# Stick-breaking attention with the queries on the partitions, on one Trainium2 core

## The chip, the cores and the metric

One NeuronCore of a Trainium2 chip runs the whole kernel. The metric is the device time of one execution in microseconds (us). Engines are named as in the profile: PE (TensorE), ACT (ScalarE), DVE (VectorE), POOL (GpSimd) and SP (SyncE, which here only issues DMAs).

## What is computed

One layer of a hybrid decoder on 1024 prompt tokens and 8 decode tokens (TT = 1032 columns), in fp32. The change lies in branch C, the stick-breaking attention of the prompt (4 heads of 128). With strict causality, key k counts for query q only where k < q:

```
z = (jnp.einsum('bqhd,bkhd->bhqk', q, k).astype(jnp.float32) * (SB_HEAD_DIM ** -0.5)
     + bias.astype(jnp.float32)[None, :, None, None])
mask = k_pos[None, :] < q_pos[:, None]
log_keep = jnp.where(mask, jax.nn.log_sigmoid(-z), 0.0)
later = lax.cumsum(log_keep, axis=3, reverse=True) - log_keep
a = jnp.where(mask, jnp.exp(jax.nn.log_sigmoid(z) + later), 0.0)
return jnp.einsum('bhqk,bkhd->bqhd', a.astype(v.dtype), v)
```

So a = sigmoid(z) times the product of sigmoid(-z) over all later keys up to the query. k and v of the prompt and of the decode tokens are outputs too. The same stage also projects the columns of branch B (a gated causal convolution of width 3) and of a merge gate.

## The kernel before, in words

The kernel is a row of stages (blocks) with a barrier after each: normalise the input, project_attention, stick_breaking_prompt, then the mLSTM, the merge and the feed-forward stages, which the change leaves alone.

*Projection.* Every projection works in blocks of 128 output columns. SP loads 512 KB of weights (load_weights), POOL splits them into a rounded part and a remainder (split_weights, L106 and L109), PE multiplies (project_chunk, L136): a block is three chunks of 344 token columns, a chunk is 24 products (8 slices of 128 input features, each as high x high, high x low, low x high). ACT copies a chunk out of PSUM. Weight buffers alternate, so the split of block n + 1 starts when block n - 1 is done.

*project_attention* (L345) projects q, k and v of four heads, 12 blocks, into s_T, feature-major.

*stick_breaking_prompt* (L423) runs over four heads (loop variable j). In a head it projects four more blocks, 12 chunks, and the 12 chunks are the slots between which the attention's own work is laid. A head has 12 units (UNITS): half 0 has key blocks 3 to 0, half 1 has 7 to 0; a unit is one block of 128 keys on the partitions by up to 512 queries. A unit goes through the engines in this order:

- PE scores (L506): z, keys on the partitions, fp32.
- ACT softplus_log (L568 to L574) and DVE softplus_parts, softplus_sum, split_softplus (L647 to L671): softplus of z, masked on the diagonal, split into a high and a low part, sp_hi and sp_lo.
- POOL add_later and split_later (L736 to L757): the running sum over the later key blocks, split too.
- PE sums (L514, L520): products with triangles and with minus ones, which add the sums of the later keys to z in PSUM.
- ACT probs (L582): exp; POOL mask_prob (L764) on diagonal units.
- PE values (L529): one fp32 product of v_tok with up to 512 columns of prob, added into y.

PE's order is written out by hand in the slot loop at L535: chunk(slot), scores(slot - 1), sums(slot - 2), values(slot - 3). A head has 15 such slots, the last three without a chunk. At slot 0 turn_kv (L486) turns the head's v and k, which ACT staged (L587, L589), token-major; they are stored from there. DVE also runs the convolution (L715, L680 to L685, L720).

## Time and profile before

| | |
|---|---|
| runs | 2289.34, 2289.61 and 2295.07 us, median 2289.61 |
| the profiled execution | span 2287.8 us from its first to its last instruction |
| PE, busy share of the span | 92% |
| DVE, ACT, POOL | 40%, 22%, 33% |
| project_attention | PE's products from 43.93 to 181.4 us |
| stick_breaking_prompt | from 184.5 us; the next stage's first product at 544.09 us |

Times in the rows are us from the span's start. A busy share says little where products overlap: the profile shows a product of 344 columns as 0.32 us long, though the next starts 0.16 us later. The waits say which engine PE stood still for, and the granted clock at which of its levels it ran.

### The profile page before, as it was taken

The numbers are of one execution on the slowest core, as the hardware profiler recorded it, in microseconds if no ns is written. First come the engines' busy times: TensorE is split into PE (matmuls) and PEld (weight loads), VectorE is DVE, ScalarE is ACT, GpSimd is POOL, SyncE is SP. The second block draws the span as 40 slices with busy tenths as digits, with TensorE's granted clock in tenths as the row PEclk, the third lists the DMA queues.
The fourth block names the chain that finished last, engine by engine and source line by source line (L and its number), as shares of the span: only waits on it lengthen the run. The fifth ranks groups of instructions, "written<-read, shape, count | busy, mean of one in ns | idle before, by whom it ended". The sixth has DMA issues, their size and how long they took to land. (4 is left out here: it accounts for less than half of the span.)

```text
span 2287.8 us, 36641 instructions
## 1 busy us (share of the span) xinstructions
PE 2112.9 (92%) x12796; PEld 2020.3 (88%) x12796; DVE 924.2 (40%) x1515; ACT 493.9 (22%) x929; POOL 760.0 (33%) x585
## 2 busy tenths in 40 slices
PE   7999798897999989996999999999999999997797
PEld 6998687686898979996899989999999999997787
DVE  3003655655346435663546443312412312344423
ACT  4113343341111112221213122101101200212321
POOL 5334564553232212220224323333333333332441
PEclk9999899998999989998889999999999999998898
DMA  6112112113343235552644402111111111111012
GB/s 187 46 37 65 53 39 64 55 28 121 98 123 111 74 120 156 156 152 85 208 148 125 148 20 64 46 46 46 46 46 46 46 46 46 46 46 49 26 39 91
DMA packets 238683, 182.41 MB, mean 80 GB/s; under 512 B 15730, under 2 KB 212474, under 8 KB 238508
## 3 DMA queue, kind: packets, MB, share of 16 engines
q1 hardware_dynamic: 221356, 158.60, 24.2%
q10 hardware_dynamic: 17280, 23.22, 2.9%
q8 instruction: 26, 0.43, 0.1%
q14 instruction: 21, 0.17, 0.0%
HBM read 147.69 MB, written 34.12 MB: 79 GB/s over the span
## 5 line engine op out<-in xcount | busy, mean ns | idle before, releaser
L136 PE MATMUL acc<-x_hi,w_hi 128*128 128x344 f32 x2688 | 887.0, 330 | 41.7 <-DVE x_lo L1867 15.7
L136 PE MATMUL acc<-x_lo,w_hi 128*128 128x344 f32 x2688 | 866.1, 322 | 0.0
L136 PE MATMUL acc<-x_hi,w_lo 128*128 128x344 f32 x2688 | 865.3, 322 | 0.0
L106 POOL TENSOR_SCALAR w_hi<-w_raw 128x1024 fp32r<-128x1024 f32 (+2 forms) x176 | 189.9, 1079 | 1275.5 <-PE acc L136 1081.9
L136 PEld LDWEIGHTS acc<-x_hi,w_hi 128*128 128x128 f32 x2688 | 512.6, 191 | 59.8 <-issue 26.1
L136 PEld LDWEIGHTS acc<-x_lo,w_hi 128*128 128x128 f32 x2688 | 511.8, 190 | 6.6 <-issue 5.4
L136 PEld LDWEIGHTS acc<-x_hi,w_lo 128*128 128x128 f32 x2688 | 511.6, 190 | 0.0
L109 POOL TENSOR_TENSOR w_lo<-w_raw,w_hi 128x1024 fp32r<-128x1024 f32 (+2 forms) x176 | 399.3, 2269 | 14.7
L136 PE MATMUL acc<-z_hi,w_hi 128*128 128x344 f32 x768 | 246.5, 321 | 0.0
L136 PE MATMUL acc<-z_hi,w_lo 128*128 128x344 f32 x768 | 245.5, 320 | 0.0
L136 PE MATMUL acc<-z_lo,w_hi 128*128 128x344 f32 x768 | 245.3, 319 | 0.0
L1812 DVE TENSOR_TENSOR h<-acc,h 128x344 f32 (+1 forms) x120 | 61.7, 514 | 310.6 <-PE acc L136 310.6
L2039 ACT ACTIVATE relu_sq<-relu 128x344 f32<-128x344 f32 x96 | 47.3, 492 | 551.5 <-DVEq L2006 551.5
L136 PEld LDWEIGHTS acc<-z_hi,w_hi 128*128 128x128 f32 x768 | 144.6, 188 | 0.2 <-issue 0.2
L136 PEld LDWEIGHTS acc<-z_lo,w_hi 128*128 128x128 f32 x768 | 144.4, 188 | 0.2 <-issue 0.2
L136 PEld LDWEIGHTS acc<-z_hi,w_lo 128*128 128x128 f32 x768 | 144.5, 188 | 0.0
L2002 DVE SCALAR_TENSOR_TENSOR relu<-acc,sq_sum 128x344 f32<-128x344 f32 x96 | 49.4, 515 | 209.1 <-PE acc L136 209.1
L136 PE MATMUL acc<-y_hi,w_hi 128*128 128x344 f32 x288 | 99.0, 344 | 32.4 <-DVE y_lo L1713 29.9
L1993 DVE TENSOR_TENSOR x_lo<-relu_sq,x_hi 128x344 f32 x96 | 95.7, 1010 | 29.4 <-issue 29.4
L136 PE MATMUL acc<-y_lo,w_hi 128*128 128x344 f32 x288 | 98.2, 341 | 0.0
L136 PE MATMUL acc<-y_hi,w_lo 128*128 128x344 f32 x288 | 97.6, 339 | 0.0
L136 PEld LDWEIGHTS acc<-y_hi,w_hi 128*128 128x128 f32 x288 | 59.3, 206 | 37.5 <-DVE y_lo L1713 22.8
(303 smaller groups left out, 2140.5 us busy)
## 6 DMA issues: line engine op xcount, KB each, us to landing
w_raw<-in_w_in SPq DMA_DIRECT2D x64, 512.0 KB, 4.3
page<-in_cache_k SPq DMA_DIRECT2D x64, 256.0 KB, 2.9
v_page<-in_cache_v SPq DMA_DIRECT2D x64, 256.0 KB, 2.7
w_raw<-in_w_up SPq DMA_DIRECT2D x32, 512.0 KB, 4.1
w_raw<-in_w_down SPq DMA_DIRECT2D x32, 512.0 KB, 3.7
merge_gate<-merge_gates SPq DMA_DIRECT2D x24, 516.0 KB, 3.8
merge_gates<-gate_out ACTq DMA_DIRECT2D x16, 516.0 KB, 3.3
y_raw<-branch_outputs SPq DMA_DIRECT2D x9, 688.0 KB, 6.7
```

The costliest lines, as they stand in the source:

```text
L106: nc.gpsimd.tensor_scalar(k.w_hi[:, par, 0:kb, :], k.w_raw[:, par, 0:kb, :], 1.0, 1.0, ALU.mult, ALU.mult).then_inc(k.w_rounded, 1)
L109: nc.gpsimd.tensor_tensor(k.w_lo[:, par, 0:kb, :], k.w_raw[:, par, 0:kb, :], k.w_hi[:, par, 0:kb, :].bitcast(F32), ALU.subtract).then_inc( ...
L136: mm = k.nc.tensor.matmul(k.acc[:, c, 0:CW], w[:, par, i, :], x[:, i, cols], start=(i == 0 and j == 0), stop=(i == kb - 1 and j == 2))
L1812: k.nc.vector.tensor_tensor(out[:, :, cols], k.acc[:, c:c + 1, 0:CW], out[:, :, cols], ALU.add).then_inc(k.acc_free, 1)
L1993: nc.vector.tensor_tensor(u_lo[:, bass.ds(i * 2 + par, 1), c * CW:(c + 1) * CW], square[:, c:c + 1, :], u_hi[:, bass.ds(i * 2 + par, 1), c ...
L2002: nc.vector.scalar_tensor_tensor(out=relu[:, c, :], in0=k.acc[:, c, 0:CW], scalar=0.0, in1=norm.rstd[:, c * CW:(c + 1) * CW], op0=ALU.max, ...
L2039: nc.scalar.activation(square[:, c, :], relu[:, c, :], ACT.Square).then_inc(s["squared"], 1)
```

## The change

Queries are put on the partitions, keys along the free dimension. A unit is now one block of 128 queries by up to four key blocks (still 12 per head, 48 in all, and the same 36 blocks of 128 by 128 per head). ACT makes keep = sigmoid(-z - bias) and beta = sigmoid(z + bias) straight from PSUM. DVE runs one scan along the keys in reversed order (a product of keep, and a maximum with a matrix that puts 1 where the mask ends), which leaves the running product in left, and multiplies beta by it. POOL masks beta on the diagonal block. PE turns the probabilities, block by block, ACT copies them out, and PE multiplies each block by v. The sums over later keys as products, the splits and the chain on POOL are gone. Units run on over the heads without a pause: PE's order per slot is chunk(slot), scores(slot + 1), turn(slot), values(slot - 1).

project_attention projects v first, then k, then q, and turns v and k of a head behind the first chunk of the next block; SP stores them from there. The loops are written out, and ACT's table for the stage holds the sigmoid.

```diff
-def project_attention(k, groups, s_T, then):
+def project_attention(k, s_T, v_tok, then):
...
+    V, KEY, Q = range(3)
+    cols = (C_SV, C_SK, C_SQ)
...
+        def place(n):
+            g, h = divmod(n, H)
+            return v_head[:, h % 2, :] if g == V else s_T[:, (g == KEY) * H + h, :]
...
+                for n in range(1, count):
+                    g, h = divmod(n, H)
+                    load_weights(k, sp, base + n, n % 2, w_in[:, :, cols[g] + h * P:cols[g] + (h + 1) * P])
+                    if 0 <= n - 3 < 2 * H:
+                        store(n - 3)
...
+                def turn(n):
+                    g, h = divmod(n, H)
+                    pe.wait_ge(k.acc_free, (base + n + 1) * NCH + NCH)
+                    if g and h == 0:
+                        pe.wait_ge(s["dec_ready"], g)
+                    tr = nc.tensor.transpose(dec[:, h * P:(h + 1) * P], place(n)[:, T:TT], k.ident[:, :])
+                    if h == H - 1:
+                        tr.then_inc(s["dec_turned"], 1)
+                    if g != Q:
+                        if n >= 2:
+                            pe.wait_ge(s["tok_ready"], n - 1)
+                        for tb in range(TB):
+                            tr = nc.tensor.transpose(turned[:, n % 2, tb // 4, (tb % 4) * P:(tb % 4 + 1) * P],
+                                                     place(n)[:, tb * P:(tb + 1) * P], k.ident[:, :])
+                        tr.then_inc(s["turned"], 1)
+                for n in range(count):
                     for c in range(NCH):
+                        project_chunk(k, pe, base + n, n % 2, c, k.x_hi, k.x_lo)
+                        if c == 0 and n:
+                            turn(n - 1)
+                turn(count - 1)
...
-            pe.wait_ge(k.acc_free, (base + H) * NCH + NCH)
-            for h in range(H):
-                tr = nc.tensor.transpose(turned[:, h * P:(h + 1) * P], s_T[:, h, T:TT], k.ident[:, :])
-            tr.then_inc(q_turned, 1)
...
+                for n in range(2 * H):
+                    g, h = divmod(n, H)
+                    dve.wait_ge(s["turned"], n + 1)
+                    if g == KEY and h >= 2:
+                        dve.wait_ge(k_out[h % 2], 16 * (h // 2))
+                    out = v_tok[:, h, :, :] if g == V else k_tok[:, h % 2, :, :]
+                    nc.vector.tensor_copy(out, turned[:, n % 2, :, :].rearrange("p a (b d) -> p (a b) d", d=P))\
+                        .then_inc(s["tok_ready"], 1)
+                    if h == H - 1:
+                        read_decode(g, kv_dec[:, g, :])
+                read_decode(Q, k.q_tok[:, :])
...
-UNITS = [(half, kb, max(0, kb * P - half * 512)) for half in range(2) for kb in range(4 * half + 3, -1, -1)]
+UNITS = [(h, i, 4 * part, min(i + 1 - 4 * part, 4)) for h in range(H) for i in range(TB) for part in range(i // 4, -1, -1)]
...
+FIRST = [kb0 == 4 * (i // 4) for _, i, kb0, _ in UNITS]
+NFIRST = [sum(FIRST[:u]) for u in range(NU + 1)]
+HALF_END = [u for u in range(NU) if UNITS[u][1] % 4 == 3 and UNITS[u][2] == 0]
...
-                with pe.Fori(0, H) as j:
-                    for slot in range(SLOTS + 3):
-                        if slot < SLOTS:
-                            b, c = divmod(slot, NCH)
-                            project_chunk(k, pe, base + j * NB + b, b % 2, c, k.x_hi, k.x_lo)
-                        if slot == 0:
-                            turn_kv(j)
-                        if 0 <= slot - 1 < NU:
-                            scores(j, slot - 1)
-                        if 0 <= slot - 2 < NU:
-                            sums(j, slot - 2)
-                        if 0 <= slot - 3 < NU:
-                            values(j, slot - 3)
...
+                def scores(u):
+                    h, i, kb, n = UNITS[u]
+                    if u >= 2:
+                        pe.wait_ge(s["beta_ready"], u - 1)
+                    nc.tensor.matmul(z[:, u % 2, 0:n * P], s_T[:, h, i * P:(i + 1) * P],
+                                     s_T[:, H + h, kb * P:(kb + n) * P], start=True, stop=True).then_inc(s["z_ready"], 1)
+                def turn(u):
+                    h, i, kb, n = UNITS[u]
+                    pe.wait_ge(s["prob_ready"], u + 1)
+                    if u >= 2:
+                        pe.wait_ge(s["copied"], u - 1)
+                    for b in range(n):
+                        tr = nc.tensor.transpose(tp[:, u % 2, b * P:(b + 1) * P], prob[:, u % 2, b * P:(b + 1) * P], k.ident[:, :])
+                    tr.then_inc(s["turned"], 1)
+                def values(u):
+                    h, i, kb, n = UNITS[u]
+                    pe.wait_ge(s["copied"], u + 1)
+                    if FIRST[u] and i % 4 == 0 and u:
+                        pe.wait_ge(s["y_read"], sum(e < u for e in HALF_END))
+                    for b in range(n):
+                        mm = nc.tensor.matmul(y[:, (i % 4) * P:(i % 4 + 1) * P], v_tok[:, h, kb + b, :],
+                                              prob_T[:, u % 2, b * P:(b + 1) * P], start=(FIRST[u] and b == 0),
+                                              stop=(kb == 0 and b == n - 1), skip_group_check=True)
+                    mm.then_inc(s["av_done"], 1)
+                scores(0)
+                for slot in range(H * SLOTS):
+                    n, c = divmod(slot, NCH)
+                    project_chunk(k, pe, base + n, n % 2, c, k.x_hi, k.x_lo)
+                    if slot + 1 < NU:
+                        scores(slot + 1)
+                    turn(slot)
+                    if slot:
+                        values(slot - 1)
+                values(NU - 1)
...
+                def sigmoids(u):
+                    h, i, kb, n = UNITS[u]
+                    act.wait_ge(s["z_ready"], u + 1)
                     if u >= 2:
+                        act.wait_ge(s["left_ready"], u - 1)
+                    nc.scalar.activation(keep[:, u % 2, 0:n * P], z[:, u % 2, 0:n * P], ACT.Sigmoid, scale=-1.0,
+                                         bias=neg_bias[:, h:h + 1]).then_inc(s["keep_ready"], 1)
                     if u >= 2:
+                        act.wait_ge(s["turned"], u - 1)
+                    nc.scalar.activation(prob[:, u % 2, 0:n * P], z[:, u % 2, 0:n * P], ACT.Sigmoid,
+                                         bias=k.b_sb[:, h:h + 1]).then_inc(s["beta_ready"], 1)
+                def copy_turned(u):
+                    h, i, kb, n = UNITS[u]
+                    act.wait_ge(s["turned"], u + 1)
+                    if u >= 2:
+                        act.wait_ge(s["av_done"], u - 1)
+                    nc.scalar.activation(prob_T[:, u % 2, 0:n * P], tp[:, u % 2, 0:n * P], ACT.Copy).then_inc(s["copied"], 1)
...
+                sigmoids(0)
+                for slot in range(H * SLOTS):
+                    n, c = divmod(slot, NCH)
+                    j, b = divmod(n, NB)
...
+                    acc_wait(k, act, base + n, c)
+                    nc.scalar.activation(proj[:, b, c * CW:(c + 1) * CW], k.acc[:, c, 0:CW], ACT.Copy).then_inc(k.acc_free, 1)
+                    if slot + 1 < NU:
+                        sigmoids(slot + 1)
+                    copy_turned(slot)
+                    if b == 0 and c == 1 and j:
+                        send_conv(j - 1)
+                    if slot - 2 in HALF_END:
+                        send_y(HALF_END.index(slot - 2))
...
+                def leave(u):
+                    h, i, kb, n = UNITS[u]
+                    lo, hi = kb * P, (kb + n) * P
+                    if u:
+                        dve.wait_ge(s["prob_ready"], u)
+                    if u % SLOTS == 0:
+                        nc.vector.memset(left[:, P:T + 1:P], 1.0)
                         dve.drain()
+                    dve.wait_ge(s["keep_ready"], u + 1)
+                    if FIRST[u]:
+                        masked, start = behind[:, 512 - n * P:512], 1.0
                     else:
+                        masked, start = behind[:, 0:1].to_broadcast([P, 512]), left[:, hi:hi + 1]
+                    nc.vector.tensor_tensor_scan(left[:, lo:hi][:, ::-1], keep[:, u % 2, 0:n * P][:, ::-1], masked[:, ::-1],
+                                                 start, ALU.mult, ALU.max).then_inc(s["left_ready"], 1)
+                    if FIRST[u]:
+                        dve.wait_ge(s["beta_masked"], NFIRST[u] + 1)
+                    else:
+                        dve.wait_ge(s["beta_ready"], u + 1)
+                    dve.wait_ge(s["left_ready"], u + 1)
+                    nc.vector.tensor_tensor(prob[:, u % 2, 0:n * P], prob[:, u % 2, 0:n * P], left[:, lo + 1:hi + 1],
+                                            ALU.mult).then_inc(s["prob_ready"], 1)
+                def read_y(e):
+                    dve.wait_ge(s["av_done"], HALF_END[e] + 1)
+                    if e >= 2:
+                        dve.wait_ge(y_sent[e % 2], 16 * (e // 2))
+                    nc.vector.tensor_copy(y_out[:, e % 2, :], y[:, :]).then_inc(s["y_read"], 1)
...
+                leave(0)
+                for slot in range(H * SLOTS):
+                    j, e = divmod(slot, SLOTS)
+                    if slot + 1 < NU:
+                        leave(slot + 1)
+                    if slot - 1 in HALF_END:
+                        read_y(HALF_END.index(slot - 1))
...
+                def mask_beta(u):
+                    h, i, kb, n = UNITS[u]
+                    pool.wait_ge(s["beta_ready"], u + 1)
+                    nc.gpsimd.affine_select(out=prob[:, u % 2, (n - 1) * P:n * P], in_=prob[:, u % 2, (n - 1) * P:n * P],
+                                            compare_op=ALU.is_gt, fill=0.0, base=0, pattern=[[-1, P]],
+                                            channel_multiplier=1).then_inc(s["beta_masked"], 1)
+                mask_beta(0)
+                for slot in range(H * SLOTS):
+                    n, c = divmod(slot, NCH)
+                    if c == 0:
+                        split_weights(k, pool, base + n + 1, (n + 1) % 2, (base + n + 1) // 2)
+                    if slot + 1 < NU and FIRST[slot + 1]:
+                        mask_beta(slot + 1)
...
-            s_T = k.sb(part, "s_T", [P, 3 * H, TT])
-            project_attention(k, [group(C_SQ, block_of(s_T, 0), HD_SCALE), group(C_SK, block_of(s_T, H)),
-                                  group(C_SV, block_of(s_T, 2 * H))], s_T, w_in[:, :, C_CC:C_CC + P])
-            stick_breaking_prompt(k, s_T, w_in[:, :, C_MQ:C_MQ + P])
+            s_T = k.sb(part, "s_T", [P, 2 * H, TT])
+            v_tok = k.sb(part, "v_tok", [P, H, TB, P])
+            project_attention(k, s_T, v_tok, w_in[:, :, C_CC:C_CC + P])
+            stick_breaking_prompt(k, s_T, v_tok, w_in[:, :, C_MQ:C_MQ + P])
```

The places where instructions move:

PE in project_attention, at the end before and behind the first chunk of the second block after. Before, the stage ends with four turns of the query's decode rows (s_T[:, h, T:TT]) and goes on to the loop of the next stage:

```order
L368 COMPARE_AND_BRANCH
L375 MATMUL q_turned<-ident,s_T 8x128 x4
L355 UNCONDITIONAL_BRANCH
L481 UNCONDITIONAL_BRANCH
L534 UNCONDITIONAL_BRANCH
L534 ISA
```

After, v_head is a head's projected v, kv_turned and rows_turned are PSUM:

```order
L136 MATMUL acc<-x_hi,w_hi 128x344
L136 MATMUL acc<-x_lo,w_hi 128x344
L136 MATMUL acc<-x_hi,w_lo 128x344
L407 MATMUL rows_turned<-ident,v_head 8x128
L414 MATMUL kv_turned<-ident,v_head 128x128 x8
L136 MATMUL acc<-x_hi,w_hi 128x344
L136 MATMUL acc<-x_lo,w_hi 128x344
```

Eight such groups, with v_head and then s_T, have come into the stage from the heads' loop.

PE between two chunks of the stick-breaking stage, in the first slot after slot 1 of the first head whose score has 128 columns. Before:

```order
L506 MATMUL z<-s_T,k_head 128x128
L512 REGISTER_ALU
L514 MATMUL z<-sp_hi,neg_from_r 128x512
L514 MATMUL z<-sp_lo,neg_from_r 128x512
L517 REGISTER_ALU
L520 MATMUL z<-later_hi,neg_ones_r 128x384
L520 MATMUL z<-later_lo,neg_ones_r 128x384
L528 REGISTER_ALU
L529 MATMUL y<-prob,v_tok 128x384
```

After (tp is the turned block in PSUM, sb_prob_T its copy):

```order
L511 MATMUL z<-s_T 128x128
L520 MATMUL tp<-ident,sb_prob 128x128 x4
L529 MATMUL y<-sb_prob_T,v_tok 128x128 x3
```

The four products with the triangle and with minus ones are gone, four turns have come, and the value is three products of 128 columns where it was one of 384.

DVE, one unit of 512 columns. Before (off the diagonal):

```order
L647 TENSOR_SCALAR z_pos<-z,sb_bias 128x512
L654 TENSOR_TENSOR z_abs<-z_pos,z_abs 128x512
L668 REGISTER_ALU
L669 CAST sp_hi<-z_abs 128x512
L671 TENSOR_TENSOR sp_lo<-z_abs,sp_hi 128x512
```

After, two units and the piece of the convolution that stands between the first and the second:

```order
L634 SCALAR_TENSOR_TENSOR sb_left<-sb_keep,sb_behind 128x384
L641 TENSOR_TENSOR sb_prob<-sb_prob,sb_left 128x384
L654 TENSOR_SCALAR proj_out<-cx,conv_w_c 128x1032
L655 COPY cx_tails<-cx 128x10
L634 SCALAR_TENSOR_TENSOR sb_left<-sb_keep,sb_left,sb_behind 128x512
L641 TENSOR_TENSOR sb_prob<-sb_prob,sb_left 128x512
```

Four passes of DVE over a unit (five on the diagonal) have become the scan and one product.

## Rows read from the trace of the kernel before

**Rows 1.** The page, part 1: busy time (share of the span) and instructions.
```profile
PE 2112.9 (92%) x12796; PEld 2020.3 (88%) x12796; DVE 924.2 (40%) x1515; ACT 493.9 (22%) x929; POOL 760.0 (33%) x585
```

**Rows 2.** Windows: stretch, length, busy PE, PEld, DVE, ACT, POOL, PE clock, DMA share, GB/s.
```profile
184.50:539.00 354.50, 307.83 (x1596) 259.98 (x1596) 210.27 (x275) 135.73 (x253) 193.25 (x216) 0.94 0.17 51
```

**Rows 3.** PE's waits, 184.5 to 544 us: total us, times, longest.
```profile
PE z L514 <- DVE sp_lo L671: 37.3, 17, 5.1
PE y L529 <- POOL prob L764: 4.8, 4, 1.2
PE z L491 <- ACT cx L589: 4.6, 3, 2.2
PE acc L136 <- DVE neg_ones_r L642: 2.6, 1, 2.6
```

**Rows 4.** Timeline, PE in head 0: start, length, operation [idle before <-releaser].
```profile
190.52 0.32 PE L136 MATMUL acc<-x_lo,w_hi 128*128 128x344 f32 x1
...
194.14 0.38 PE L506 MATMUL z<-s_T,k_head 128*128 x2
...
216.40 0.38 PE L506 MATMUL z<-s_T,k_head 128*128 x2
...
218.24 0.32 PE L136 MATMUL acc<-x_lo,w_hi 128*128 128x344 f32 x1
...
256.54 1.02 PE L506 MATMUL z<-s_T,k_head 128*128 x2
...
257.85 0.39 PE L520 MATMUL z<-later_hi,neg_ones_r 128*128 128x512 f32 x1
258.08 0.40 PE L520 MATMUL z<-later_lo,neg_ones_r 128*128 128x512 f32 x1
...
259.17 1.02 PE L506 MATMUL z<-s_T,k_head 128*128 x2
```

**Rows 5.** Timeline, PE: turns of a head's v; weight loads of fp32 products, input stage.
```profile
188.40 1.03 PE L491 MATMUL z<-ident,cx 128*128 128x128 f32 x8
189.27 0.27 PE L493 MATMUL z<-ident,cx 128*8 128x128 f32 x1
...
16.96 1.86 PEld L334 LDWEIGHTS pt_s<-x_scales,x_rows 128*128 128x128 f32 x16 [1.62 <-DVE x_scales L292]
18.74 0.91 PEld L326 LDWEIGHTS pt_x<-ident,x_rows 128*128 128x128 f32 x8
```

**Rows 6.** Timeline, DVE and POOL in head 0.
```profile
237.15 0.69 DVE L671 TENSOR_TENSOR sp_lo<-z_abs,sp_hi 128x512 fp32r<-128x512 f32 x1
...
243.55 2.40 POOL L109 TENSOR_TENSOR w_lo<-w_raw,w_hi 128x1024 fp32r<-128x1024 f32 x1
243.78 2.72 DVE L671 TENSOR_TENSOR sp_lo<-z_abs,sp_hi 128x512 fp32r<-128x512 f32 x1
```

**Rows 7.** Timeline, the end of the last head and the next stage's first product.
```profile
529.33 0.63 PE L514 MATMUL z<-sp_lo,neg_from_r 128*128 128x512 f32 x1
...
538.78 0.69 DVE L692 COPY y_stick<-y 128x512 f32<-128x512 f32 x1 [0.92 <-PE y L529]
...
544.09 0.65 PE L136 MATMUL acc<-x_hi,w_hi 128*128 128x344 f32 x1 [4.91 <-PEq L463]
```

**Rows 8.** Groups (count, busy us, mean ns) of ACT and POOL; one DVE instruction, timeline.
```profile
L568 ACT ACTIVATE z_abs<-z,sb_bias 128x512 f32<-128x512 f32 x24 | 16.5, 688 | 8.2 <-PE z L506 8.0
L603 ACT ACTIVATE proj_out<-acc 128x344 f32<-128x344 f32 x48 | 21.9, 457 | 139.5 <-PE acc L136 122.6 <-issue 16.9
L764 POOL TENSOR_SCALAR_AFFINE_SELECT prob<-prob 128x128 f32<-128x128 f32 x32 | 13.4, 418 | 0.0
...
270.68 3.38 DVE L683 SCALAR_TENSOR_TENSOR proj_out<-cx,conv_w_c,proj_out 128x1024 f32<-128x1024 f32 x1
```

**Rows 9.** Timeline, PE: the first product of two stages.
```profile
43.93 0.65 PE L136 MATMUL acc<-x_hi,w_hi 128*128 128x344 f32 x1 [2.03 <-PEq L229]
...
184.52 0.42 PE L136 MATMUL acc<-x_hi,w_hi 128*128 128x344 f32 x1 [2.57 <-DVE neg_ones_r L642]
```

More of the change, by code:

```diff
@@ L444, in stick_breaking_prompt @@
-        later_lo = k.sb(ctx, "later_lo", [P, 512], F32R)
-        neg_from = k.sb(ctx, "neg_from_r", [P, P], F32R)
-        neg_ones = k.sb(ctx, "neg_ones_r", [P, P], F32R)
-        later = k.sb(ctx, "sp_later", [P, 512])
-        prob = k.sb(ctx, "prob", [P, 2, 512])
-        y_out = k.sb(ctx, "y_stick", [P, T])
+        keep = k.sb(ctx, "sb_keep", [P, 2, 512])
+        prob = k.sb(ctx, "sb_prob", [P, 2, 512])
+        left = k.sb(ctx, "sb_left", [P, T + 2])
+        prob_T = k.sb(ctx, "sb_prob_T", [P, 2, 512])
@@ L463, in stick_breaking_prompt @@
+        y_sent = [k.sem(ctx, f"sb_y_sent{i}") for i in range(2)]
         with nc.Block() as block:
@@ L634, in _ @@
+                send_conv(H - 1)
+                send_y(2 * H - 1)
+                for i in range(2):
+                    act.wait_ge(y_sent[i], 16 * H)
+                act.wait_ge(s["conv_sent"], 16 * H)
+                act.wait_ge(s["gate_sent"], 16 * H)
             @block.vector
             def _(dve):
[L636 to L639 removed]
```

411 lines of the change are left out of this document (107 added, 304 removed).

## The prediction

> **What bounds the kernel now.** The page comes first: TensorE (PE) is busy 92% of the span of 2287.8 us [rows 1], so only time in which PE waits, runs at its lower clock or does work that can be dropped is worth anything. Both stages that the change touches lie before 544.09 us. The windows show the stick-breaking stage: from 184.5 to 539 us, 354.5 us, PE is busy 307.83 us at a mean granted clock of 0.94 [rows 2]. The waits name what holds it [rows 3]: 37.3 us in 17 waits of the sums (L514) for sp_lo from DVE, 4.8 us for the mask on POOL, 4.6 us for the staged head, and before the stage 2.6 us for a constant. The rest of the gap is the clock: a 128x512 product that takes 0.39 us takes 0.63 us at 529.33 [rows 4, 7], after PE had waited for sp_lo. A mean of 0.94 between 1.0 (2.4 GHz) and 0.5 (1.2 GHz) is 12% of 354.5 us at the lower level, half of which is lost: 21 us.
>
> **Prices on PE**, all at the higher level.
> - Projection: 23 products from 190.52 to 194.14 [rows 4], 0.1574 us each; a chunk of 24 is 3.78 us.
> - 512 columns: a single-pass product is 0.23 us (257.85 to 258.08). The unit from 256.54 to 259.17, 2.63 us, has four of these and two fp32 ones (score and value) [rows 4]; (2.63 - 0.92) / 2 = 0.85 us, or 0.21 per 128 columns.
> - Turning a 128x128 block: eight from 188.40 to 189.27 [rows 5], 0.109 us each.
> - An fp32 product of 128 columns that loads its own weights: eight pairs of loads from 16.96 to 18.74 [rows 5], 0.2225 us each.
> - Coming back to the projection: from 216.40 to 218.24 less one product of 0.157 is 1.68 us; the parts (score 0.21, sums 0.46, later sums 0.35, value 0.64) make 1.66 [rows 4]. So 0.02; I take 0.1 per slot for the new kinds, which change weights every 128 columns, and keep 0 and 0.2 as ends.
>
> A head has 12 units, 36 blocks of 128 keys by 128 queries, before and after. Before, its extra PE work is 36 x (0.21 + 0.21) = 15.3, sums 36 x 2 x 0.058 = 4.2, later sums 28 x 2 x 0.058 = 3.2, turning k and v about 2.0 and 0.2 for returns: 25, with 12 chunks 70.4. Four heads: 281 us. With the waits inside the stage (46.7) and the clock (21) that makes 349 of the 354.5 us, so nothing large is missing.
>
> **The change, part by part.**
> 1. *Stick stage, PE.* Sums and later sums go; 36 blocks are turned; a value product is now one per block. Per head: 36 x 0.2125 + 36 x 0.109 + 36 x 0.2225 + 12 x 0.1 = 7.7 + 3.9 + 8.0 + 1.2 = 20.8 us. With chunks: 4 x (45.4 + 20.8) = 264.6 us.
> 2. *The wait in each slot.* turn(u) needs prob(u). PE issues scores(u) at the end of slot u - 1, then turn(u - 1), values(u - 2), a whole chunk and scores(u + 1) before turn(u). For 512 columns that cover is 0.44 + 0.89 + 3.78 + 0.85 = 5.9 us; its smallest value for such a unit (u = 3, between narrow ones) is 0.33 + 0.45 + 3.78 + 0.21 = 4.8. The chain under it: keep on ACT 0.69 [rows 8], the scan, the product with left 0.69 (the 128x512 operation at 237.15 [rows 6]), and about 0.4 for three or four hand-overs; beta (0.69) runs beside the scan. The scan is in no row. From below it is the 0.69 us of a two-input operation over 512 [rows 6]; from above I take the longest two-input operation shown, 3.38 us over 1024 columns while POOL split weights [rows 8]. That gives a chain of 2.5 to 5.2. I take 1.0 for the scan, nearest its low end since operands and length are those of the short row: chain 2.8, no wait. Only in the four narrow places could the top end show, 0.4 us each. The Trainium skill (DVE: opcode table, instruction layouts, handler registers and perf-mode slots, section 6, Datapath and trigger behaviour) says that the built-in scan runs at half throughput; as an estimate from it the scan is some 1.3 us, and the sum stays what it is. No run here shows it yet.
> 3. *What else is queued.* ACT per slot: projection copy 0.46 [rows 8], two sigmoids and the copy of the turned block, at most 0.46 + 3 x 0.69 = 2.5 us, against 5 us or more of PE. send_conv, send_y and the gates only issue DMAs whose work is finished slots earlier. DVE: the convolution pieces and read_y come behind leave(u + 1), whose result is due about 4 us later. POOL loses its chain and keeps the weight splitting and eight masks per head. SP's loads keep their order. All this I cost at nothing; its cover is the chunk of 3.78 us.
> 4. *Ends of heads.* Before, each head drains its pipeline in three slots without a chunk, and those waits are in rows 3. After, units run on across heads, and the pipeline drains once; values(46), 0.89 us, covers the last copy.
> 5. *Exit.* From the last copy of y (538.78) to the next stage's first product (544.09) is 5.31 us [rows 7]; this chain (copy, tails, two small stores, barrier) stays. With 0.3 us from the last value product: 5.6.
> 6. *Attention stage.* Eight k/v blocks are turned there: 8 x (8 x 0.109 + 0.11) = 7.9; the query rows 0.3 more; 11 returns of 0.1: 1.1. The last turn now waits for ACT's last copy (0.46 us [rows 8]), in place of the four turns that stood at the end: even. Sum +9.3. turn(n - 1) stands behind chunk 0 of block n, so the copies it needs are done by then; stores of k and v now queue on SP between weight loads that are due two blocks later.
> 7. *Stage start.* 2.57 us of idleness that ended with neg_ones_r [rows 9] becomes a plain stage change, 2.03 us in the place before the attention stage, plus the first score 0.2: -0.3.
>
> **Sum.** From the first projection product at 184.52 to 544.09 is 359.6 us; now 264.6 + 5.6 = 270.2. -89.4 + 9.3 - 0.3 = **-80.4 us**. The profiled span of 2287.8 becomes 2207.4; the median of the runs, 2289.6, lies 1.8 above the span, so **2209 us**.
>
> **The rivals.**
> *A. POOL holds the scans.* In every third slot the split of the next weights starts when a block ends, just as that slot's unit goes through DVE. The trace shows what this does: the same operation takes 0.69 us at 237.15 and 2.72 beside the split at 243.78 [rows 6]. If scan and product are both held so, each 2.0 us longer, and the mask (0.4 [rows 8]) stands between them, the chain is 2.8 + 4.4 = 7.2 us against 5.9: 1.3 us in each of 16 slots, 21 us, **2230**. For it: both new operations read two SBUF operands, as the held one does. Against it: the split is 3.4 us long in all, so two full holds hardly fit, and the chain's first 0.8 us is ACT's. The Trainium skill (SBUF — State Buffer, Who interferes with whom) states that such a DVE instruction and a GpSimd one that reads SBUF shut each other out for the whole instruction; by that rule A is real, and the row at 243.78 agrees with it.
> *B. The scan is serial and slow; slower than before.* Its elements depend on one another, and it may run far below the rate of a product. A head has six units of 512 columns, the stage 24. Their scan may take 1.0 + (5.9 - 2.8) = 4.1 us before PE waits at all; the gain is gone when each of them waits 80.4 / 24 = 3.35 us, so from a scan of 7.5 us, eleven times the short row. At 9 us, 24 x 4.9 = 118 us come on top: **2327**. PE would idle in front of the turns.
> *C. Straight-line code.* The PE stream has 4530 rows for 2927, since the loops are written out. If fetching it cost the 2.03 us of a stage change [rows 9] once in each of 28 blocks, 57 us return: **2266**. Against it: head 0 runs its body for the first time at 0.1574 us a product.
>
> **How the numbers follow.** Forecast 0.75; A 0.17; C 0.04; B 0.04. About 0.3% (7 us) is what a measurement of this kernel can tell from no change. B is slower: 0.04. A code price 1.4 times C's (80 us) would end within 0.3%: 0.01 of C's share. The rest is faster: 0.95. The forecast's own range: returns of 0 to 0.2 us (4.8 either way) and some 3 us for exit and start, 2201 to 2217. Taking in A with the mask stretched too (to 2238), leaving out B and C: **2200 to 2238**.
>
> **What would show it.** In the new profile: no wait of turn (L520) on sb_prob above 0.5 us; a granted clock of 0.99 from start to end of the stage, and a stage of 265 us from its first score to its last value; the attention stage about 9 us longer; scans of 512 at 0.7 to 1.5 us away from the split. A shows as scans of 2 us or more beside the split, with PE idle in every third slot. B shows as DVE busy without a gap. C shows as PE idle for no releaser, in straight runs of projection. I am wrong if waits at L520 or L529 come to over 30 us, or if the stage exceeds 300 us.

## The result, and the profile after

The change makes the kernel faster: the median is 2195.92 us (2193.39 to 2198.25, 4 runs) against 2289.48 of the kernel before, a ratio of 0.9583, 95% interval 0.9569 to 0.9596. The forecast was 2209, its range 2200 to 2238. Sign and mechanism came out as argued. The size did not: the gain is 93.6 us where the sum had 80.4, and the time lies 4 us under the low end of the range.

PE is the page's first line, to be set beside [rows 1]:

```profile
PE 2073.3 (94%) x12956; PEld 2011.6 (92%) x12956; DVE 846.3 (39%) x1390; ACT 448.0 (20%) x869; POOL 637.8 (29%) x433
```

The windows view, over the attention stage and over the stick-breaking stage from its first projection product to the copy of its last y (columns as in [rows 2]):

```profile
44.00:192.00 148.00, 146.35 (x941) 145.18 (x942) 11.71 (x12) 16.64 (x37) 41.25 (x24) 0.99 0.26 72
192.09:452.40 260.31, 260.31 (x1682) 244.18 (x1682) 119.60 (x142) 90.67 (x193) 73.35 (x64) 1.00 0.18 54
```

In the second stretch PE is busy for 260.31 of 260.31 us, at a granted clock of 1.00, its upper level of 2.4 GHz. In [rows 2] it was 307.83 of 354.5 at 0.94. From the first projection product to the copy of the last y the stage took 354.3 us before (184.52 to 538.78 [rows 7, 9]) and takes 260.3 now, 93.9 less. Of these, 46.7 are the waits inside the stage [rows 3], and some 20 the lower clock, an estimate from the mean of 0.94, of which about 2 fell into waits. The rest, some 29, is PE work that was dropped or has moved to the attention stage. PE's waits between 40 and 480 us, in place of [rows 3] (total us, times, longest):

```profile
PE acc L136 <- PEq L493: 3.7, 1, 3.7
PE z L511 <- PEq L367: 1.0, 1, 1.0
PE acc L136 <- PEq L229: 0.9, 1, 0.9
PE rows_turned L407 <- ACT s_T L451: 0.5, 1, 0.5
```

No wait at the turns (L520) or the value products (L529) is in the list. What remains are changes of stage and the turn of the last query rows. Next the timeline: the turns of two successive blocks in the attention stage, the stage's start, and its exit (rows of several engines between them left out).

```profile
60.82 1.03 PE L414 MATMUL kv_turned<-ident,v_head 128*128 128x128 f32 x8
...
73.14 1.03 PE L414 MATMUL kv_turned<-ident,v_head 128*128 128x128 f32 x8
...
191.88 0.46 PE L511 MATMUL z<-s_T 128*128 128x128 f32 x2 [1.04 <-PEq L367]
...
192.09 0.40 PE L136 MATMUL acc<-x_hi,w_hi 128*128 128x344 f32 x1
...
452.41 0.69 DVE L648 COPY y_stick<-y 128x512 f32<-128x512 f32 x1 [3.38 <-PE y L529]
...
456.47 0.42 PE L136 MATMUL acc<-x_hi,w_hi 128*128 128x344 f32 x1 [3.66 <-PEq L493]
```

And the groups of DVE in the stage (count, busy us, mean ns, idle before):

```profile
L634 DVE TENSOR_TENSOR_SCAN sb_left<-sb_keep,sb_left,sb_behind 128x512 f32<-128x512 f32 x16 | 28.2, 1764 | 55.2 <-ACT sb_keep L559 55.2
L641 DVE TENSOR_TENSOR sb_prob<-sb_prob,sb_left 128x512 f32<-128x512 f32 x24 | 20.0, 832 | 2.6
...
L634 DVE TENSOR_TENSOR_SCAN sb_left<-sb_keep,sb_behind 128x512 f32<-128x512 f32 x8 | 9.8, 1225 | 16.3 <-ACT sb_keep L559 16.3
```

The scan, which no row of before showed, takes 1.23 us over 512 columns, or 1.28 for one that continues a row. The mean of 1764 ns over the 16 continuing ones is above that because four of them, one in each head, ran beside POOL's split of the weights and took 3.20. The one of the first head, with the product and the turn of its unit:

```profile
238.80 2.39 POOL L109 TENSOR_TENSOR w_lo<-w_raw,w_hi 128x1024 fp32r<-128x1024 f32 x1
...
239.06 3.20 DVE L634 TENSOR_TENSOR_SCAN sb_left<-sb_keep,sb_left,sb_behind 128x512 f32<-128x512 f32 x1 [3.23 <-ACT sb_keep L559]
...
242.37 0.69 DVE L641 TENSOR_TENSOR sb_prob<-sb_prob,sb_left 128x512 f32<-128x512 f32 x1
...
243.94 0.60 PE L520 MATMUL tp<-ident,sb_prob 128*128 128x128 f32 x4
```

The scan beside the split of the weights ends (242.26) 1.07 us after the split (241.19), so most of its own 1.28 us ran behind it. PE doesn't notice: the turn of this unit stands behind a whole chunk and comes 0.9 us after the product has ended (243.06). That time between the product's end and the turn is the slack of a unit. Read from the same timeline, it is 1.9 to 3.7 us in 39 of the 48 units, 0.9 in eight (in each head the two units of 512 columns whose scan or product meets the split), and 0.2 in the stage's second unit.

Where the forecast missed, piece by piece (us; before from [rows 7, 9]):

| piece | forecast | measured | difference |
|---|---|---|---|
| shift of the stage's first projection product (184.52 to 192.09) | +9.0 | +7.6 | -1.4 |
| from there to the copy of the last y | 264.9 | 260.3 | -4.6 |
| exit to the next stage's first product (452.41 to 456.47) | 5.31 | 4.06 | -1.25 |
| later stages (456.47 to the end) | 1743.7 | 1740.0 | -3.7 |
| median of the runs against the profiled span | +1.8 | -0.6 | -2.4 |

The differences sum to -13.4, the miss (13.1) within rounding. The last line is the choice of the execution that was profiled: it took 2198.25 us, the longest of the four. The experiments ask which of them are real, and whether the mechanism is the one that was forecast. "Stage" below is the time from the first score (191.88) to the start of the copy of the last y (452.41), 260.5 us in the changed kernel; "time" is a median of all runs of that kernel.

### The profile page after: what moved, and what is told of

Its sections match the earlier page's. It is cut to its first block and busy times, and to the rows that moved or that the text cites. A ratio compares the mean times of both kernels' runs of the same rounds, so it can differ in the third digit from the quotient of the medians.

```text
span 2196.5 us, 35629 instructions
## 1 busy us (share of the span) xinstructions
PE 2073.3 (94%) x12956; PEld 2011.6 (92%) x12956; DVE 846.3 (39%) x1390; ACT 448.0 (20%) x869; POOL 637.8 (29%) x433
## 5 line engine op out<-in xcount | busy, mean ns | idle before, releaser
L106 POOL TENSOR_SCALAR w_hi<-w_raw 128x1024 fp32r<-128x1024 f32 (+2 forms) x176 | 184.5, 1048 | 1292.1 <-PE acc L136 1096.3
L109 POOL TENSOR_TENSOR w_lo<-w_raw,w_hi 128x1024 fp32r<-128x1024 f32 (+2 forms) x176 | 398.7, 2265 | 14.7
```

The source lines that it names most:

```text
L106: nc.gpsimd.tensor_scalar(k.w_hi[:, par, 0:kb, :], k.w_raw[:, par, 0:kb, :], 1.0, 1.0, ALU.mult, ALU.mult).then_inc(k.w_rounded, 1)
L109: nc.gpsimd.tensor_tensor(k.w_lo[:, par, 0:kb, :], k.w_raw[:, par, 0:kb, :], k.w_hi[:, par, 0:kb, :].bitcast(F32), ALU.subtract).then_inc( ...
```

## The experiments

| kernel | time (runs) | ratio to before, 95% | stage | waits in the stage, last waited-for |
|---|---|---|---|---|
| changed, again (again) | 2195.92 (5) | 0.9561 to 0.9591 | 260.6 | none |
| scans twice (scan2) | 2199.24 (4) | 0.9574 to 0.9608 | 263.0 | 0.9, turns for DVE |
| scans three times (scan3) | 2223.47 (4) | 0.9690 to 0.9724 | 290.3 | 20.4, turns for DVE |
| scans four times (scan4) | 2266.19 (4) | 0.9867 to 0.9901 | 329.8 | 45.1, turns for DVE |
| values in mid-chunk (returns2) | 2208.33 (5) | 0.9619 to 0.9650 | 271.5 | 8.4 for the copy of y, 0.7 for ACT |
| scores in mid-chunk (returns2b) | 2195.77 (5) | 0.9574 to 0.9602 | 260.7 | none |
| no turns, values a slot early (no_turn) | 2225.56 (5) | 0.9695 to 0.9722 | 283.1 | 22.4 for the copy of y |
| no turns, values in place (no_turn2) | 2183.77 (5) | 0.9521 to 0.9549 | 244.7 | none |
| heads drained (head_drain) | 2195.88 (5) | 0.9577 to 0.9610 | 260.9 | none |
| late store of y (late_y) | 2197.09 (5) | 0.9575 to 0.9601 | 260.6 | none |
| before, no remainders in the sums | 2281.11 (5) | 0.9942 to 0.9969 | | 43.9 for sp_lo, 7.7 for POOL |
| before, no taps | 2275.92 (5) | 0.9920 to 0.9947 | | 25.5 for sp_lo, 7.5 for POOL |

### Scatter: the changed kernel again

The edit is none.

> The changed kernel once more. The forecast was 13 us too high: 7.2 us of it lie before the next stage's first product, 3.7 us in later stages, 2.3 us in the choice of the profiled run. Theory 1: the 7.2 us are real and return: first projection product of the stage at 192.1, next stage's first product at 456.5 us, each within 0.7. Theory 2: they are scatter of single runs: the two numbers move by 3 us or more. The 3.7 us of the later stages I take for scatter: from 456.5 to the end 1738 to 1743 us. Time 2193 to 2198 us.

Measured: the median is the same to the hundredth. Theory 1 holds for the lengths: stage 260.6 us (192.81 to 453.38), exit 4.06. The two places, 193.03 and 457.44, are both 0.9 later, just beyond the 0.7 that was allowed, because the attention stage's first product comes later (45.17 in place of 44.06). From 457.44 to the end it took 1739.8 us. That last figure comes out of every profile here, since all kernels share the later stages: in the fourteen profiles it runs from 1735.9 (late store of y) to 1743.7 (the kernel before), and one variant of the changed kernel has 1743.5. So 3.7 us lie within the scatter between single executions, with the one profile of before at its top. That all of it is scatter is not shown: the three profiles of the kernel before and its variants average 1742.5 us, the eleven of the changed kernel and its variants 1739.2. Single runs of the kernel before, 27 beside these experiments, went from 2284.94 to 2295.93.

### What is the bound: turns left out

```diff
...
-                    pe.wait_ge(s["copied"], u + 1)
+                    pe.wait_ge(s["prob_ready"], u + 1)
...
                     if slot + 1 < NU:
                         scores(slot + 1)
-                    turn(slot)
-                    if slot:
-                        values(slot - 1)
-                values(NU - 1)
+                    values(slot)
...
-                    copy_turned(slot)
...
```

> The changed kernel without turning the probabilities: no turns on PE, no copies of turned blocks on ACT; the value products read prob as it stands, so y is computed from probabilities that aren't turned. 144 turned blocks at 0.109 us are 15.7 us of PE work. Theory (PE is the bound of the stage, at the higher clock without a gap): the time falls by 15.7 us, within 2, and the waits of PE stay under 2 us. Rival (the slots are paced by the chain through ACT and DVE, PE only looks busy): it falls by under 5 us and PE waits at the value products.

Measured: 29.6 us slower instead of 15.7 faster. The edit had moved the value products one slot forward, and there they meet another wait. PE's waits in the stage:

```profile
PE y L529 <- DVE y_stick L644: 22.4, 7, 3.7
PE z L511 <- PEq L367: 1.0, 1, 1.0
```

y is one buffer; the first values of a half need the copy of the last half, and DVE takes that copy only after the next unit's scan and product. The changed kernel leaves a slot between. Neither theory was tested by this run, but it shows what such a wait costs. PE's timeline, and windows before, in and after the first wait:

```profile
220.81 0.76 PE L529 MATMUL y<-sb_prob,v_tok 128*128 128x128 f32 x2 [3.66 <-DVE y_stick L644]
```

```profile
208.00:215.90 7.90, 7.90 (x55) 7.90 (x54) 3.73 (x4) 1.23 (x4) 4.85 (x4) 1.00 0.20 55
216.00:221.00 5.00, 1.34 (x5) 0.54 (x5) 2.58 (x3) 1.72 (x3) 0.00 (x0) 0.86 0.04 12
221.00:228.00 7.00, 7.00 (x30) 6.95 (x31) 0.00 (x0) 0.37 (x1) 0.00 (x0) 0.61 0.01 2
```

After 3.66 us of idleness the mean granted clock of a busy PE is 0.61 over the 7 us from 221 on, most of it at the lower level. Against the 244.7 us that the stage takes without the turns (next run) it is 38.4 us longer, for 22.4 us of waits.

The same without the flaw, with the value products where they were (the wait for prob_ready as above):

```diff
...
-                    turn(slot)
                     if slot:
                         values(slot - 1)
...
-                    copy_turned(slot)
...
```

> no_turn again without its flaw (there the value products came a slot earlier and waited 22.4 us for the copy of y): turns and copies of turned blocks are left out, the value products stay a slot behind and read prob as it stands, so y is computed from probabilities that aren't turned. Theory (PE is the bound): minus 15.7 us within 2, no waits at the value products. Rival (chain-bound): under minus 5 us, with waits.

Measured: the stage falls by 15.8 us (192.03 to 436.74), with no wait. PE work counts one to one in the new stage: it is PE-bound. The time falls by 12.2, short of the 15.7 within 2: 0.5 us are in the exit (4.56), the other 3 within what the rest of the program varies by.

### How far the cover reaches: scans two, three and four times

```diff
+        extra = k.sb(ctx, "sb_extra", [P, 1, 512])
...
+                    for x in range(1):
+                        nc.vector.tensor_tensor_scan(extra[:, x, 0:n * P][:, ::-1], keep[:, u % 2, 0:n * P][:, ::-1], masked[:, ::-1],
+                                                     start, ALU.mult, ALU.max)
                     nc.vector.tensor_tensor_scan(left[:, lo:hi][:, ::-1], keep[:, u % 2, 0:n * P][:, ::-1], masked[:, ::-1],
...
```

(2 and 3 in place of the two 1s for three and four scans.)

> Every scan is issued twice (the first copy into a spare buffer that nothing reads). This adds about 47 us of DVE work over 48 units. Theory (a chunk of PE covers the chain): the chain of a 512 unit grows from 3.1 to 4.4 us, under the cover of 4.8 to 5.9 us, so the time stays within 4 us of the changed kernel; what shows is in the slots whose scan POOL's split holds. Rival (DVE's chain is the pace of a slot): the time grows by 31 to 47 us.

> Every scan is issued four times (three copies into spare buffers that nothing reads); 142 us more DVE work. Theory (cover): the chain of a 512 unit is 0.7 + 4 x 1.28 + 0.7 + 0.4 = 6.9 us against 5.9 us of cover (4.8 in four places), so PE waits at the turns about 1 us in 20 units and 2 us in four, 28 us, with holds by POOL and the convolution up to 60; the waits are at the turn, released by the DVE product. Rival (DVE's work is paid one to one): plus 142 us. Second rival (deeper slack than I count, the two buffers of prob let PE run on): under 10 us.

> Every scan three times (two copies into spare buffers that nothing reads). scan4 waited 45.1 us at the turns, eight times 3.25 to 4.42 us, and took 69.6 us more: after each long wait the granted clock fell. With one scan less each of these waits shrinks by 1.28 us: 18 to 20 us of waits remain, nearly all in two units per head. Theory (a wait costs itself and the clock behind it): 20 to 38 us more than the changed kernel. Rival (a wait costs only itself, and what scan4 took beyond its waits was something else that goes with DVE work): the time beyond the waits is two thirds of scan4's 24.5 us whatever the clock shows.

Measured with two: the stage is 2.5 us longer, for 44.8 us more of DVE (166.25 against 121.47 in the repeat, between 192.1 and 455). The cover theory holds. With four: plus 69.3 us in the stage, beyond my 28 to 60, and less than half of the 153 us by which DVE's busy time in the stage grew (272.41 against 119.60). PE's waits at the turns were 45.1 us, as the theory had them:

```profile
PE tp L521 <- DVE sb_prob L645: 45.1, 29, 4.4
```

The other 24 us are not waits in this list. PE's timeline around the longest wait, and windows of the stage and of this place:

```profile
217.82 1.12 PE L521 MATMUL tp<-ident,sb_prob 128*128 128x128 f32 x4 [4.42 <-DVE sb_prob L645]
...
220.59 0.49 PE L136 MATMUL acc<-x_hi,w_lo 128*128 128x344 f32 x1
220.88 0.49 PE L136 MATMUL acc<-x_hi,w_hi 128*128 128x344 f32 x1
...
223.90 0.32 PE L136 MATMUL acc<-x_hi,w_lo 128*128 128x344 f32 x1
224.05 0.32 PE L136 MATMUL acc<-x_hi,w_hi 128*128 128x344 f32 x1
```

```profile
192.81:522.75 329.94, 284.74 (x1683) 259.50 (x1684) 272.41 (x288) 93.03 (x193) 88.58 (x64) 0.94 0.14 43
213.00:225.00 12.00, 7.58 (x35) 7.39 (x34) 6.33 (x8) 1.57 (x4) 4.06 (x2) 0.72 0.16 44
```

After the wait a projection product starts every 0.29 us, later every 0.155 again. A mean clock of 0.94 over 329.9 us is some 20 us, of which 2 fell into the waits themselves: some 18 of the 24. With three scans the waits are 20.4 us and the longest 3.1; the mean clock is 0.99 (about 3 us), and the stage is 29.8 us longer. So the clock's share fell with the long waits, as its theory had it, and the rival's 16 us beyond the waits did not come. Of the 9.4 us that did, the clock is only a third: it fell with two of the four waits of 3.1 us (the stretches from 216.3 and from 288.0) and stayed at 1.00 with the others. The remaining 6 us, the same in both runs, lie mostly at the turns. Each of these stages has the same 1682 PE records as the changed kernel's, so they can be set record by record beside it. With four scans the starts that wait come 49.8 us later in sum, those at the lower clock 16.7 and the others 2.8; with three it is 22.6, 2.9 and 4.3. A wait thus took some 0.16 us more than the idle time shown, which fits that a product is drawn past the start of a next one that needn't wait. What went beyond the slack cost about 1.5 times the wait (69.3 for 45.1, 29.8 for 20.4).

### The price of a return

```diff
...
-                    project_chunk(k, pe, base + n, n % 2, c, k.x_hi, k.x_lo)
...
+                    project_chunk(k, pe, base + n, n % 2, c, k.x_hi, k.x_lo, between=between)
                     if slot + 1 < NU:
                         scores(slot + 1)
                     turn(slot)
-                    if slot:
-                        values(slot - 1)
```

(`between` issues values(slot - 1) after 12 of the chunk's 24 products.)

> The value products of a slot move from the end of the slot into the middle of its chunk, after 12 of 24 products: PE now leaves the projection and comes back twice per slot, 47 more returns, with the same products. My sum took 0.1 us per return (0 to 0.2). Theory 1 (a return costs nothing): the time stays within 1 us of the changed kernel. Theory 2 (0.1 us each): plus 4.7 us. Theory 3 (0.2): plus 9.4 us. If a wait for the copy of the turned block (1.9 us of products cover turn and copy) showed instead, it would stand at the value products in the list of waits.

Measured: the stage is 11.0 us longer, but 9.1 us of it are waits: 8.4 for the copy of y, the place that no_turn met too, and 0.7 for ACT. The other 1.9 over 47 returns are at most 0.04 us each, for returns from value products, one of the new kinds that the sum priced. The cleaner form moves scores(slot + 1) into the middle instead:

> A cleaner price of a return than returns2, whose moved value products waited 8.4 us for the copy of y. Here the score of the next unit moves into the middle of the chunk, and turn and values stay behind it: 47 more returns to the projection, the same products, and no earlier need of any engine's result. Theory (a return costs nothing, or the 0.04 us left over in returns2): the stage is 0 to 2 us longer than the 260.3 us from first projection product to the copy of y, with no waits. Rival (0.1 us, as my sum had it): plus 4.7 us.

Measured: no waits, the stage 0.2 us longer, the time 2195.77. A return from a score costs 0.2 / 47 = 0.004 us: nothing. Theory holds, the 0.1 of the sum falls.

### The exit

```diff
-                    if slot - 2 in HALF_END:
+                    if slot - 2 in HALF_END[:-2]:
                         send_y(HALF_END.index(slot - 2))
...
+                send_y(2 * H - 2)
                 send_y(2 * H - 1)
```

> The last head's first half of y is stored at the end, right ahead of the second half, so 512 KB of y leave at the stage's exit, as before the change, in place of 256 KB. The exit took 4.06 us from the last copy of y to the next stage's first product, where the kernel before took 5.31. Theory (the amount stored at the end sets it): the exit is 5.0 to 5.5 us, the whole time 1.2 us longer, which the runs can hardly tell. Rival (the rest of the exit sets it): 4.0 to 4.2 us.

Measured: the copy of the last y starts at 452.97, the next stage's first product at 457.89, so the exit is 4.92 us. That is 0.86 of the 1.25 us by which the exit had shrunk, just under the theory's 5.0 and well above the rival's 4.2: less data stored last shortens it. The amount of y is not all. In no_turn 256 KB of y are stored last as in the changed kernel, but the store is issued 0.75 us behind that of the convolution in place of 2.14, and the exit took 5.63 us.

### What held the kernel before, and the ends of heads

```diff
-                    for part in (sp_hi, sp_lo):
+                    for part in (sp_hi,):
...
-                        for part in (later_hi, later_lo):
+                        for part in (later_hi,):
```

> The kernel before, with the products of the remainders sp_lo and later_lo left out of the sums on PE (only the rounded parts are summed; DVE and POOL still make the remainders). This takes 64 products per head with 0.058 us per 128 columns, 14.8 us in all, off PE. Theory (before, PE waits for DVE in these slots, so PE work there is in part free): the time falls by 3 to 10 us and the waits for sp_lo grow. Rival (PE work counts one to one in the kernel before as well): minus 14.8 us.

Measured: minus 10.1 us of the 14.8, at the edge of what I had expected; the waits of the sums grew from 37.3 [rows 3] to 43.9, those for POOL from 4.8 to 7.7, and the mean clock of the stage fell from 0.94 to 0.92. The stage itself, from its first projection product to the copy of its last y, took 347.4 us (185.84 to 533.28) in place of 354.3, only 6.8 less. So in the kernel before, a third (by the time) to half (by the stage) of the PE work taken away came back as waits and lower clock; in the changed one nothing did.

```diff
-                        if u > 8:
-                            convolve(j, 11 - u)
+                        if u == 9:
+                            dve.wait_ge(s["cx_ready"], j + 1 + 1)
+                            nc.vector.tensor_copy(tails[:, bass.ds(j, 1), :], cx[:, T:T + 2 + B].unsqueeze(1))
+                            dve.drain()
```

> The kernel before, with the three taps of branch B's convolution left out on DVE (the products with B and C gates and the tails stay). The waits of the sums for sp_lo were 37.3 us, longest where pieces of the convolution lie between two units on DVE. Theory (DVE's queue, with pieces held by POOL, makes sp_lo late): the waits fall by 15 us or more, the clock follows, and the time falls by 20 to 45 us. Rival (the serial chain of abs, exp, log, sum, split itself is longer than the cover): the waits stay above 30 us and the time falls by under 8 us.

Measured: minus 15.3 us, between the two theories; the waits for sp_lo fell to 25.5, by 11.8 and not by 15, and stayed under the rival's 30. Its timeline of PE in head 0:

```profile
247.05 0.50 PE L514 MATMUL z<-sp_hi,neg_from_r 128*128 128x512 f32 x1 [1.54 <-DVE sp_lo L671]
...
262.96 0.69 PE L514 MATMUL z<-sp_hi,neg_from_r 128*128 128x512 f32 x1 [3.51 <-DVE sp_lo L671]
...
268.46 0.50 PE L520 MATMUL z<-later_hi,neg_ones_r 128*128 128x512 f32 x1 [1.35 <-POOL later_lo L759]
```

The 3.5 us wait stands in every head, convolution or not, right behind the head's last chunk. With the taps in place a second wait follows it, of 2.0 to 5.1 us. The timeline of the kernel before, for its first two heads:

```profile
263.70 0.50 PE L514 MATMUL z<-sp_hi,neg_from_r 128*128 128x512 f32 x1 [3.50 <-DVE sp_lo L671]
...
270.81 0.80 PE L514 MATMUL z<-sp_hi,neg_from_r 128*128 128x512 f32 x1 [5.06 <-DVE sp_lo L671]
...
351.26 0.79 PE L514 MATMUL z<-sp_hi,neg_from_r 128*128 128x512 f32 x1 [3.50 <-DVE sp_lo L671]
...
356.67 0.50 PE L514 MATMUL z<-sp_hi,neg_from_r 128*128 128x512 f32 x1 [2.04 <-DVE sp_lo L671]
```

The other two heads have 3.51 with 2.03 and 3.51 with 2.04. So 25 of the 37.3 us stood at the ends of heads, where no chunk covers what DVE still has to do: 14.0 for the serial chain of abs, exp, log, sum and split of the last unit but one, and 11.2 where the taps of the convolution stand in DVE's queue as well, since these waits for sp_lo went with the taps. The chain itself was stretched by POOL. Timeline of the kernel before, DVE and POOL ahead of the wait that ends at 263.70:

```profile
259.45 1.26 POOL L757 TENSOR_TENSOR later_lo<-sp_later,later_hi 128x512 fp32r<-128x512 f32 x1 [0.16 <-issue]
...
259.64 1.62 DVE L654 TENSOR_TENSOR z_abs<-z_pos,z_abs 128x512 f32<-128x512 f32 x1 [0.57 <-ACT z_abs L574]
...
261.37 1.27 POOL L739 TENSOR_TENSOR sp_later<-sp_later,z_abs 128x512 f32<-128x512 f32 x1 [0.66 <-DVEq L662]
261.47 1.45 DVE L669 CAST sp_hi<-z_abs 128x512 fp32r<-128x512 f32 x1 [0.21 <-DVEq L662]
```

Without the taps, in the next unit (263.67 and 264.57), where POOL stood still, the same two passes of DVE took 0.69 and 0.43 us. So about 1.95 us of each 3.5 us wait, in all four heads, is DVE held beside the running sum on POOL, which the change removes. No run here takes that hold away by itself. Is it the running on over heads, or this shorter chain, that gains in the changed kernel?

```diff
...
+                    drain = slot % SLOTS == SLOTS - 1
-                    if slot + 1 < NU:
+                    if slot + 1 < NU and not drain:
                         scores(slot + 1)
                     turn(slot)
-                    if slot:
+                    if slot % SLOTS:
                         values(slot - 1)
-                values(NU - 1)
+                    if drain:
+                        values(slot)
+                        if slot + 1 < NU:
+                            scores(slot + 1)
...
```

(On ACT, at these slots, the copy of the turned block goes ahead of the next unit's sigmoids.)

> The changed kernel, but at the end of each head the pipeline is drained: the last values wait for the last copy before the next head's first score is issued. Three inner heads' ends get a wait of a turned block's copy (0.6 to 0.69 us on ACT and two hand-overs), about 1.2 us each. Theory (the new chain has so little left at a head's end that running on across heads is worth little): plus 3 to 6 us, waits at the value products 3 to 5 us. Rival (running on is where the kernel before lost: its drains took 3.5 us and 2.0 to 5.1 us of waits per head): plus 15 us or more.

Measured: 2195.88 us, the stage 0.4 us longer, no wait at all. Both theories miss. The timeline of the first drained end:

```profile
255.06 0.60 PE L520 MATMUL tp<-ident,sb_prob 128*128 128x128 f32 x4
...
255.50 2.01 PE L529 MATMUL y<-sb_prob_T,v_tok 128*128 128x128 f32 x16
255.70 0.60 ACT L575 ACTIVATE sb_prob_T<-tp 128x512 f32<-128x512 f32 x1
257.34 0.39 PE L511 MATMUL z<-s_T 128*128 128x128 f32 x2
```

The unit's value products wait for the 0.60 us copy, but those of the unit before it (the first half of the 16 instructions, 0.89 us) cover that, and all run on without a gap. Running on over heads is worth nothing by itself here. The ends of heads cost nothing now because what is left to do behind the last chunk is one copy, not a chain through ACT, DVE and POOL.

## Where the forecast held, and where it failed

- **Bound and mechanism: right.** The forecast took PE as the limit once the waits were gone. The stage shows PE 100% busy at a clock of 1.00, and taking 15.7 us of its work away takes 15.8 off.
- **The step that failed** is the price of "coming back to the projection": the sum took 0.1 us per slot where its own row gave 0.02, on the ground that the new kinds change weights every 128 columns. Measured it is 0.004 behind a score and at most 0.04 behind value products. The attention stage shows the same behind turns: a block lasts 73.14 - 60.82 = 12.32 us, and 72 x 0.1574 + 0.11 + 8 x 0.109 = 12.31 leaves nothing for a return. Items 1 and 6 were 4.8 and 1.1 us too high by this; without it they give 259.8 us to the last value product, 260.1 with the 0.3 from there to the copy of y, where 260.3 was measured, and +8.2.
- **Item 5** was taken over whole (5.31 us); it fell to 4.06, and the late store of y gives 0.86 of that back.
- **The range** held the bounds of the costs but not the scatter: its low end of 2200 left room for returns (4.8 of the 5.9 us of them in the sum) and for exit and start, while the stages that the change doesn't touch took 1735.9 to 1743.7 us in single executions. Without the price of a return the forecast would have been 2203, with the measured exit 2202. The other 6 us (3.7 in the later stages, 2.4 in the choice of the profiled execution) lie within the scatter, and that they all fell to the low side is chance as far as the runs show.
- **Item 2: right, with the scan mis-sized.** It was taken at 1.0 us and took 1.23 to 1.28, inside the bounds of 0.69 to 3.38; the chain stayed under the cover, and twice the scan still did but for 0.9 us of waits. The Trainium skill (DVE: opcode table, instruction layouts, handler registers and perf-mode slots, section 6, Datapath and trigger behaviour) states half throughput for the built-in scan; the trace about agrees, 1.28 us beside 0.69 for a product of the same length.
- **Rival A: its mechanism is there, its price is not.** The scan at 239.06 took 3.20 us beside the split. But its unit met one such hold, not two, and no other unit met two. Over the stage the 512 units lose 7.7 us to holds of the scan (28.2 less 16 x 1.28) and 3.4 to holds of the product (20.0 less 24 x 0.69), about 1.9 and 0.8 once per head. Both units kept 0.9 us of slack, so a second hold of 1.9 us on either would have shown. The Trainium skill (SBUF — State Buffer, Who interferes with whom) has these two shutting each other out, and the row agrees but for 0.2 us (1.07 us after the split, where the scan takes 1.28).
- **Rivals B and C: not seen.** The scan is 1.28 us, not 7.5 or more; PE is busy all through the stage, the straight runs of projection too.
- **Item 4: right in effect, not in its reason.** The waits at the ends of heads are gone, but draining the changed kernel at each head's end costs nothing either.

## What to carry to other kernels

Count what PE must wait for behind the last piece of covering work, since 25 of 37 us of waits stood there, and see whether another engine stretches it, before reordering around it. Where waits were long, a stage grew by 1.5 to 1.7 times their sum (69.3 for 45.1, 29.8 for 20.4, 38.4 for 22.4), in part because the granted clock fell with most waits of 2.6 to 4.4 us. With single waits of 1.3 us (scans four times) and 1.7 us (values in mid-chunk) it stayed at 1.00; in the kernel before it fell once, from 248.3 to 255.1 us, with two waits of 1.53 and 1.20 us that stood 1.2 us apart, and in the other three heads it did not. Where a row gives a price, take the row's value, and put the scatter of untouched stages into the range as well as the bounds of the costs.

## What the runs showed that was not expected

- A one-operand copy of ten columns is held beside POOL as a scan is. With four scans the copy of the tails fell beside the split (252.02, POOL's L109 at 251.63 for 2.71 us):

```profile
L659 DVE COPY cx_tails<-cx 128x10 f32<-128x10 f32 x4 | 9.4, 2355 | 0.0
```

  The four copies took 2.36 us each on average. In the changed kernel the same copy takes 0.168 us.
- Leaving work out made the kernel slower: 15.7 us less on PE, moved a slot forward, came out 29.6 us longer, through seven waits of up to 3.7 us and the clock behind them.
